# A two-layer encoder trunk on one core: mean squares as columns, and four modulation products beside the norms

## The reference

```python
mod = silu(c) @ mod_w[i] + mod_b[i]              # 1024 -> 6 * 1024
sh1, sc1, g1, sh2, sc2, g2 = split(mod, 6)
h = rms_norm(x, g) * (1 + sc1) + sh1
x = x + g1 * mixer(h)                            # layer 0: sparse attention; layer 1: S5 state space, GELU, GLU
h = rms_norm(x, g') * (1 + sc2) + sh2
x = x + g2 * (silu(gate) * val) @ w_down         # val, gate: causal convolution (width 3) of h @ w_up, 2816 channels each
```

## Time and profile before

| | us |
|---|---|
| timed runs | 835.84, 837.55, 838.05 |
| median | 837.55 |
| span of the profiled execution | 833.9 |
| TensorE busy | 757.5 (91%) |
| TensorE weight load busy | 681.9 (82%) |
| VectorE busy | 579.9 (70%) |
| ScalarE busy | 389.2 (47%) |
| GpSimd busy | 209.6 (25%) |

### The profile page before, as it was taken

The page is one execution under the profiler, slowest core; times in us unless marked ns, Lnnn a source line. Parts: engine busy times, 40 slices in busy tenths (PEclk is TensorE's granted clock), DMA queues, the critical chain, the costliest instruction groups (busy, mean ns, idle before and its releaser), DMA issues.

```text
span 833.9 us, 17636 instructions
## 1 busy us (share of the span) xinstructions
PE 757.5 (91%) x6676; PEld 681.9 (82%) x6676; DVE 579.9 (70%) x935; ACT 389.2 (47%) x651; POOL 209.6 (25%) x121
## 2 busy tenths in 40 slices
PE   4588999999877888999999968997999999999996
PEld 0177999558666877999999958997988999999995
DVE  7854655995689998565565787567657766666775
ACT  2255544555333434444544724332556555555553
POOL 6900000211899995000001063364000000000000
PEclk9789999999859989999999969999998999999998
DMA  8869555696315646677866412110552555555521
GB/s 310 344 222 387 180 177 177 252 407 264 138 44 208 225 153 220 237 276 264 276 254 239 149 51 77 53 53 28 190 187 79 181 197 176 181 177 189 183 101 52
DMA packets 45978, 157.51 MB, mean 189 GB/s; under 512 B 6256, under 2 KB 7792, under 8 KB 45936
## 3 DMA queue, kind: packets, MB, share of 16 engines
q1 hardware_dynamic: 43632, 148.55, 51.5%
q10 hardware_dynamic: 1728, 6.29, 1.9%
q0 software_dynamic: 576, 2.10, 0.7%
HBM read 155.87 MB, written 1.05 MB: 188 GB/s over the span
## 4 chain that ended last, share of the span: by engine, by line
PE 71%; DVE 18%; ACT 4%; issue 3%; DMA 2%; POOL 1%; DVEq 0%; ACTq 0%; POOLq 0%
PE up L326 12%; PE up L328 12%; PE up L327 12%; PE acc L326 8%; PE acc L327 8%; PE acc L328 8%; DVE wlo L978 4%; DVE hl L1007 3%; PE gv L362 3%; DVE ffn L1237 2%; DMA ffn<-in_mw 1%; DVE ffn L1232 1%; ACT whi L719 1%; DVE diag L999 1%; PE misc L373 1%
## 5 line engine op out<-in xcount | busy, mean ns | idle before, releaser
L978 DVE TENSOR_TENSOR wlo<-raw,whi 128x1024 fp32r<-128x1024 f32 x194 | 256.2, 1332 | 117.8 <-ACT whi L719 116.6
L326 PE MATMUL up<-hh,whi 128*128 128x256 f32 x944 | 276.2, 293 | 16.2 <-DVE hl L1007 10.8
L327 PE MATMUL up<-hl,whi 128*128 128x256 f32 x944 | 272.3, 288 | 0.0
L328 PE MATMUL up<-hh,wlo 128*128 128x256 f32 x944 | 272.1, 288 | 0.0
L719 ACT ACTIVATE whi<-raw 128x1024 fp32r<-128x1024 f32 x194 | 201.1, 1051 | 50.2 <-PE up L328 25.2
L326 PEld LDWEIGHTS up<-hh,whi 128*128 128x128 f32 x944 | 186.2, 197 | 30.3 <-DVE wlo L978 14.0
L327 PEld LDWEIGHTS up<-hl,whi 128*128 128x128 f32 x944 | 186.9, 198 | 0.0
L328 PEld LDWEIGHTS up<-hh,wlo 128*128 128x128 f32 x944 | 186.6, 198 | 0.0
L1232 DVE SCALAR_TENSOR_TENSOR ffn<-up,conv,ffn 128x254 f32<-128x254 f32 (+1 forms) x176 | 72.6, 474 | 55.3 <-ACT ffn L853 55.3
L326 PE MATMUL acc<-ah,whi 128*128 128x256 f32 x352 | 102.1, 290 | 8.0 <-DVE wlo L978 8.0
L327 PE MATMUL acc<-al,whi 128*128 128x256 f32 x352 | 101.8, 289 | 0.0
(11 more groups left out here) (200 smaller groups left out, 947.0 us busy)
## 6 DMA issues: line engine op xcount, KB each, us to landing
raw<-in_w SPq DMA_DIRECT2D x194, 512.0 KB, 4.1
mraw<-in_mw SPq DMA_DIRECT2D x60, 512.0 KB, 6.1
arena<-in_mw SPq DMA_DIRECT2D x12, 512.0 KB, 10.8
tmp<-in_mw SPq DMA_DIRECT2D x6, 512.0 KB, 7.9
ffn<-in_mw SPq DMA_DIRECT2D x6, 512.0 KB, 8.5
tmp<-in_mw ACTq DMA_DIRECT2D x4, 512.0 KB, 7.4
ffn<-in_mw ACTq DMA_DIRECT2D x4, 512.0 KB, 9.6
mraw<-in_mw ACTq DMA_DIRECT2D x4, 512.0 KB, 14.6
```

The lines of the kernel that those rows point to most:

```text
L326: pe.matmul(out, w_h, xh, start=first, stop=False, skip_group_check=skip)
L327: pe.matmul(out, w_h, xl, start=False, stop=False, skip_group_check=skip)
L328: return pe.matmul(out, w_l, xh, start=False, stop=last, skip_group_check=skip)
L978: dve.tensor_tensor(wlo[:, n % SPL, :], raw[:, n % RAW, :], whi[:, n % SPL, :].bitcast(F32), ALU.subtract).then_inc(lo_ready, 1)
```

## The change

The mean squares: instead of rows of sums, each squared tile is now the stationary operand. For each half of 128 tokens it is multiplied by one column that holds 1/1024 everywhere (the new small input mean), and the eight tiles are added up in two columns of misc. The row copy on ScalarE, the turning products and their two semaphores are gone. TensorE's waits for the columns of the modulation now stand ahead of the sums.

The products: 14 runs within norm 1 between the sums and the spread, 15 after the spread; 22 and 23 do the same at norm 3. Product 15 has a place of its own in the arena (fill), loaded when attention has ended; 22 and 23 are loaded after the state space (mraw and late). The loop of layer 0 has a product in its first six iterations only, 16 to 21. The sets of columns move along: one stands ahead of each layer's loop. GpSimd waits for product 15 before it writes over its place.

```diff
+C_LAST = 2 * CH - 2
+FILLED = C_LAST - C_FFN - 2
 ...
 # SP
             load_att(C_FFN)
-            for n in range(W_OUT + RAW, W_FFN0 + RAW):
+            load_w(W_OUT + RAW)
+            for s in range(MS):
+                if s == 0:
+                    sp_.wait_ge(act_lo, 2 * KT)
+                sp_.dma_start(fill[:, s, :], t["mw"][(C_FFN + 1) * MS + s, :, :]).then_inc(m_fill[s], 16)
+            for n in range(W_OUT + RAW + 1, W_FFN0 + RAW):
                 load_w(n)
-            with sp_.Fori(0, 9) as i:
+            with sp_.Fori(0, FILLED) as i:
                 for n in range(W_FFN0 + RAW, W_FFN0 + 2 * RAW):
                     load_w(n, i)
-                load_m(C_FFN + 1, i)
+                load_m(C_FFN + 2, i)
 ...
+            for s in range(2 * MS):
+                if s == 0:
+                    sp_.wait_ge(y_done, KT)
+                sp_.dma_start(mraw[:, s, :] if s < MS else late[:, s - MS, :],
+                              t["mw"][C_LAST * MS + s, :, :]).then_inc((m_loaded if s < MS else m_fill)[s % MS], 16)
 ...
 # TensorE
-            def norm(n, pairs, spread, meanwhile=None):
-                pe.wait_ge(gm_ready, pairs)
+            def norm(n, spread, meanwhile=None):
+                pe.wait_ge(cols_done, 1 if n == 0 else C_FFN // 2 if n == 1 else CH - 1 if n < 4 else CH)
+                pe.wait_ge(mod_col, 1 if n == 0 else C_FFN // 2 if n == 1 else CH - 1 if n < 4 else CH)
                 for k in range(KT):
                     pe.wait_ge(sq_ready, KT * n + k + 1)
-                    mm = pe.matmul(gv[32 * (k % 4):32 * (k % 4) + 1, 0:T], ones[:, 0:1], tmp[:, k, :],
-                                   start=(k < 4), stop=(k >= 4))
+                    for h in range(2):
+                        mm = pe.matmul(misc[:, 8 + h:9 + h], tmp[:, k, h * P:(h + 1) * P], mean[:],
+                                       start=(k == 0 and h == 0), stop=(k == KT - 1), skip_group_check=True)
                 mm.then_inc(ssum, 1)
-                pe.wait_ge(sum_row, n + 1)
-                pe.wait_ge(mod_col, pairs)
-                for h in range(2):
-                    mm = pe.matmul(misc[:, 8 + h:9 + h], gm[:, h * P:(h + 1) * P], picks[:, 0:1], start=True, stop=True)
-                mm.then_inc(csum, 1)
                 if meanwhile:
                     meanwhile()
 ...
-            norm(1, C_FFN // 2, misc[:, T:2 * T])
+            norm(1, misc[:, T:2 * T], lambda: gemv(C_FFN))
+            gemv(C_FFN + 1)
 ...
+                columns(C_FFN // 2 if layer == 0 else CH - 1)
                 if layer == 0:
-                    with pe.Fori(0, 5) as i:
-                        gemv(C_FFN, i)
+                    with pe.Fori(0, FILLED // 2) as i:
+                        gemv(C_FFN + 2, i)
                         two_steps(2 * i)
-                        gemv(C_FFN + 1, i)
+                        gemv(C_FFN + 3, i)
                         two_steps(2 * i + 1, i)
+                    with pe.Fori(FILLED, 10) as i:
+                        two_steps(i)
 ...
-            norm(3, CH, misc[:, T:2 * T])
+            norm(3, misc[:, T:2 * T], lambda: gemv(C_LAST))
+            gemv(C_LAST + 1)
 ...
 # ScalarE, root
-                act.wait_ge(cols_done, 1 if norm == 0 else C_FFN // 2 if norm == 1 else CH)
-                act.activation(gm[:, 0:T], gv[:, 0:T], ACT.Copy).then_inc(sum_row, 1)
-                act.wait_ge(csum, norm + 1)
-                act.activation(rt[:], misc[:, 8:10], ACT.Sqrt, scale=1.0 / D, bias=epsc[:, 0:1]).then_inc(rt_ready, 1)
+                act.activation(rt[:], misc[:, 8:10], ACT.Sqrt, bias=epsc[:, 0:1]).then_inc(rt_ready, 1)
 ...
 # GpSimd
+                if k == 1:
+                    pool.wait_ge(mod_used, (C_FFN + 2) * MS)
 ...
-            pool.wait_ge(mod_used, 2 * CH * MS)
+            pool.wait_ge(mod_used, C_LAST * MS)
```

More of the change, by code:

```diff
@@ L182, in build @@
         qkv_f = arena[:, 0:N_IN * T]
+        fill = arena[:, 12288:16384].rearrange("p (s n) -> p s n", n=1024)
+        late = arena[:, 0:4096].rearrange("p (s n) -> p s n", n=1024)
         hh_f = hh[:].rearrange("p k t -> p (k t)")
@@ L202, in build @@
         m_early = [sem(f"m_early{j}") for j in range(3 * MS)]
-        sum_row, csum = sem("sum_row"), sem("csum")
+        m_fill = [sem(f"m_fill{j}") for j in range(MS)]
         x_in = sem("x_in")
@@ L297, in _ @@
             load_att(C_FFN)
-            for n in range(W_OUT + RAW, W_FFN0 + RAW):
+            load_w(W_OUT + RAW)
[4 more added lines that the diff above has]
+            for n in range(W_OUT + RAW + 1, W_FFN0 + RAW):
                 load_w(n)
-            with sp_.Fori(0, 9) as i:
+            with sp_.Fori(0, FILLED) as i:
                 for n in range(W_FFN0 + RAW, W_FFN0 + 2 * RAW):
                     load_w(n, i)
-                load_m(C_FFN + 1, i)
-            for n in range(W_FFN0 + 10 * RAW, W_FFN0 + 11 * RAW):
-                load_w(n)
-            for n in range(W_SIN, W_SIN + 3):
-                load_w(n)
-            first = W_SIN + 3
+                load_m(C_FFN + 2, i)
+            with sp_.Fori(FILLED, 10) as i:
+                for n in range(W_FFN0 + RAW, W_FFN0 + 2 * RAW):
+                    load_w(n, i)
+            for n in range(W_SIN, W_GLU + 8):
+                load_w(n)
+            for s in range(2 * MS):
[3 more added lines that the diff above has]
+                              t["mw"][C_LAST * MS + s, :, :]).then_inc((m_loaded if s < MS else m_fill)[s % MS], 16)
+            first = W_GLU + 8
             loops = (N_SLOTS - first) // RAW
@@ L346, in gemv @@
                     src = mraw[:, s, :]
-                    if c >= C_FFN:
-                        pe.wait_ge(m_loaded[s], 16 * (c - C_FFN // 2 + 2 * i))
+                    if c in (C_FFN + 1, C_LAST + 1):
+                        src = (fill if c == C_FFN + 1 else late)[:, s, :]
+                        pe.wait_ge(m_fill[s], 16 if c == C_FFN + 1 else 32)
+                    elif c == C_FFN:
+                        pe.wait_ge(m_loaded[s], 16 * (c // 2))
+                    elif c > C_FFN:
+                        pe.wait_ge(m_loaded[s], 16 * (c - C_FFN // 2 - 1 + 2 * i))
                     elif c == 0:
@@ L431, in _ @@
             columns(0)
-            norm(0, 1, None)
+            norm(0, None)
             gemv(2)
@@ L608, in _ @@
             lag_kernels(range(0, 5))
-            norm(2, CH, misc[:, T:2 * T], lambda: lag_kernels(range(5, KT - 1)))
+            norm(2, misc[:, T:2 * T], lambda: lag_kernels(range(5, KT - 1)))
             lag_kernels(range(KT - 1, KT)).then_inc(k_done, 1)
@@ L707, in _ @@
             pe.wait_ge(set_up, 5)
-            norm(3, CH, misc[:, T:2 * T])
+            norm(3, misc[:, T:2 * T], lambda: gemv(C_LAST))
+            gemv(C_LAST + 1)
             ffn_phase(1, W_FFN1, 5)
-            norm(4, CH, misc[:, T:2 * T])
+            norm(4, misc[:, T:2 * T])
         @block.scalar
@@ L899, in ffn_phase @@
                 for h in range(2):
-                    step(h, 20 + h, base + 60 + 3 * h, 0, 4 if layer == 0 and h == 0 else None)
+                    step(h, 20 + h, base + 60 + 3 * h)
             act.wait_ge(small_in, 16 * N_SMALL)
@@ L1271, in two_steps @@
                         step(h, 2 * i + 2 + h, base + 6 + 3 * h, i, extra if h else None)
+                col_out(C_FFN // 2 if layer == 0 else CH - 1)
                 if layer == 0:
-                    with dve.Fori(0, 4) as i:
+                    with dve.Fori(0, FILLED // 2) as i:
                         two_steps(2 * i)
                         two_steps(2 * i + 1, i)
-                    two_steps(8)
+                    with dve.Fori(FILLED, 9) as i:
+                        two_steps(i)
                 else:
@@ L1281, in ffn_phase @@
                 for h in range(2):
-                    step(h, 20 + h, base + 60 + 3 * h, 0, 4 if layer == 0 and h else None)
+                    step(h, 20 + h, base + 60 + 3 * h)
                 if layer == 0:
@@ L1566, in layout @@
         "ones": np.ones((P, P), f),
+        "mean": np.full((P, 1), 1.0 / D, f),
         "picks": np.stack([np.arange(P) % 32 == 0, np.arange(P) % 32 == 1], axis=1).astype(f),
```

18 lines of the change are left out of this document (11 added, 7 removed).

## The result

The changed kernel takes 894.0 us (median of four runs, 893.49 to 895.72) against 836.7 (835.36 to 838.05) for the kernel before, timed beside it: a ratio of 1.069, 95% interval 1.067 to 1.071, or 57.3 us more. The forecast was 892, range 866 to 907. Its profiled execution has a span of 893.9, that of before 833.9.

What follows compares the result with a forecast made beforehand. TensorE's sequence of matmuls plus its waits was taken as the bound. Stalls 60, products -7.3 and norms +2.1 gave +54.8 on the 833.9 span, 888.7; with 3.65 around it 892.35, say 892 us, range 866 to 907.

Steps and rivals of the forecast that it cites:

- stalls in six iterations: Layer 0's feed-forward loop: TensorE waits for late product loads, 36 us in iterations 3 to 5, 24 in 0 to 2: +60.
- four products out of the loop: Layer 0's loop, iterations 6 to 9: four fewer products of 1.83 us on TensorE's chain give back 7.3 us.
- norms: All five norms with column sums: -0.9 at norm 1, -0.5 at 3, +0.8, +0.2 and +2.5 at 2, final and 0; +2.1.
- moved loads: End of attention and after the state space: loads moved past others are covered, 0 us, at most 2 if served late.
- The clock's price: Layer 0's loop: after each stall TensorE restarts at 1.2 GHz, costing 2 us each, bounds 0 and 2.9.
- the strict reading of the lock: Norm 0: VectorE and GpSimd exclude each other for whole instructions, costing 4.5 us instead of 2.5; time 894.
- the loads come in time: Rival, layer 0's loop: SP is an iteration ahead, stalls vanish, 832 us; decided by a lead of 8 us; chance 0.07.
- The shorter stalls: Rival, layer 0's loop: loads land quicker while TensorE is still and the clock holds, 36 us, 866 to 870; chance 0.14.
- No cover in the early iterations: Rival, layer 0's first iterations: VectorE is the bottleneck, delays come on top, 60 + 15, about 907 us; chance 0.08.
- The idle times: Sign in layer 0's first six iterations: TensorE idle before the products until transfers into mraw land, 8 to 12 us each.
- the iterations of 30 and 17.5 us: Sign in layer 0's loop: iterations of about 31 us, then four of about 17.5.
- A clock of 0.5 behind each stall: Sign in layer 0's loop: TensorE's granted clock would be 0.5 behind each stall.

Runs made afterwards that it cites:

- experiment 1: The changed kernel with product 16 loaded ahead of SP's loop and 17 + i in iteration i, restoring the lead: 840.1 us, ratio 1.004.
- experiment 5: Kernel before with products moved, lead restored, norms by rows, plus two weight slots issued ahead of SP's wait for attention's end: 827.6 us, ratio 0.988.
- experiment 4: Two kernels against the one before: only the new column sums, 843.7 us; only the products moved, lead restored and norms by rows, 831.0 us.
- the first group: The first of three groups in which the eleven follow-up kernels ran, each beside the kernel before, whose median there was 836.3 us.
- experiment 7: experiment 1 with norm 0's sums in another PSUM bank, ahead of the wait for the columns: 836.5 us, ratio 0.999 to the kernel before.
- experiment 3: The changed kernel with the product's four loads behind five, three or none of SP's six weight slots: 870.9, 843.6 and 841.7 us.
- behind three slots: The changed kernel with the product's loads behind three of SP's six weight slots in layer 0's loop: 843.6 us, ratio 1.008.

## Why the prediction was right, and where it was not

The mechanism is right: the kernel got slower because SP's product loads lost their iteration of lead. That the total was only 2 us off is luck. The stalls were put 6 to 7 us too high, the norms 7 and the moved loads 3 too low, and these errors nearly cancelled.

| term | forecast | trace of the changed kernel | difference of kernels |
|---|---|---|---|
| stalls in six iterations | +60 | +53.1 | +53.9 (experiment 1) |
| four products out of the loop | -7.3 | -8.5 | -8.6 (experiment 5, with all the moved work) |
| norms | +2.1 | +10.5, with products 14 and 22 in them | +9.1 (experiments 1 and 4; +7.3 alone) |
| moved loads | 0, at most 2 | | +3.3 (experiments 4 and 5) |

The last column sums to 57.7 against 57.3, but that confirms nothing: its terms are steps from one kernel to the next, from the changed kernel back to the one before, and add up to the whole whatever each is due to. The 0.4 is the difference between the medians of the kernel before, beside the changed kernel and in the first group.

**The stalls, over by 7.** For iterations 3 to 5 I forecast 12 each: 9.8 idle and 2 for the clock behind it. They cost 10.8, 10.5 and 9.7. The product ended at arrival + 12.4, against the forecast 11.6, so the place and the landing were right. The clock's price was in the wrong place: it fell on the product, while the pieces trickled in, and was largely hidden under the wait for the last piece. The slots behind it cost nothing: in all six iterations the granted clock is 1.00 there. One row was misread for it: the matmul of 0.39 us still ran at full clock, 1.00 from 268.3 to 269.0. At full clock the first matmul of a slot shows 0.38 (406.10), at half clock 0.58 (297.69). In iteration 0 the error has the other sign: 15.4 instead of 8.6. The product ended 14.0 us later than it would have (277.8, arrival 262.0, less 1.8), and nothing covered it: a wait for VectorE as long as the one that I had set against it, 4.28 us, stands at 297.69, later in the iteration. VectorE had not worked on while TensorE stood. From 274.7 to 282.04 it waited 7.33 us for a split of ScalarE's, which waited for TensorE to use a slot; before, its longest such wait in the iteration was 0.5. Iterations 1 and 2 then cost only 2.3 and 4.4 instead of 8.6 and 7. GpSimd does work on while TensorE stands: of the 63.6 us that it had left, the first iteration holds 39.9 and the third none, where before the three had 25.1, 27.5 and 16.6. So the cover lay in the next two iterations, which had been slow beside GpSimd and no longer were. The three together: 22.1 against 24.2, and this agreement too is luck.

**The products, right.** The last four iterations gave 8.5. Two sets of columns of 0.95 us also left them, which I had booked as zero since they go elsewhere: 7.3 + 1.9 would be 9.2.

**The norms, under by 7.** I assumed that sums whose squares come one by one run one by one too, so that in norms 1 and 3 only the last tile would count. TensorE does its instructions in order, and the sums stand behind the last projection. At norm 3 all 32 run in one burst of 3.63 us, which ends 2.0 us after the last square; the old chain needed 1.76 from there to the root, so the 1.08 us won with the row copy went back. At norm 1 they were won: 28 of the 32 end before the last square, which is late there, and the root starts 0.69 us behind the square instead of 1.76. But product 14 ran at half clock (3.46 us) and held the spread until 231.32, though the diagonals were ready at 229.02. The price of a burst was right (forecast 3.5 at full clock and 7 at half, measured 3.6 and 6.95), but norms 2 and 4 ran theirs at a clock of 0.90 and 0.79, in 4.1 and 4.5. Norm 0 had +2.5 and measured +4.6. It was the strict reading of the lock that came true. The Trainium skill, SBUF: State Buffer, section Two separate sides, has a GpSimd instruction and a VectorE instruction that uses the shared ports (one in a 2-port mode or with two inputs from SBUF) exclude each other for whole instructions. The diagonals agree: they end within 0.3 us of GpSimd's instruction in both kernels, and experiment 7 shows the price from the other side. The table load of 1.28 us was a term that I did not have. Before, it ran while TensorE waited for the first columns; after, it stands in the open.

**The moved loads, under by 3.** I named the cover (seven slots with their weights) and did not count when ScalarE wants the eighth: it waited 5.08 us. The second price came through TensorE's clock at norm 1, which the traces of experiment 5 show.

**The rivals.** That the loads come in time fell with the first row of waits; its condition, a lead of 8 us, is what experiment 3 found (7.3 us ahead left 1.5 us, 9.0 left 0.2). The shorter stalls by the figures of the Trainium skill (DMA: Bandwidth & Descriptors, Anatomy of one DMA) did not occur: the transfers took what the trace before had shown, 6.8 to 7.3 us for the fourth, and the stalls of iterations 3 to 5 cost 9.7 to 10.8. No cover in the early iterations fell as well, but only for the three together: they cost 22.1 us, where three uncovered ones would cost some 31 at the price of the later iterations. The first alone had no cover.

**The signs.** The idle times came, 5.1 to 10.4 us where 8 to 12 were named, and the iterations of 30 and 17.5 us. A clock of 0.5 behind each stall came only in the product. The loop became 44.6 us longer (53.1 less 8.5) instead of some 50.

Open: why three of the kernels with column sums (experiments 1 and 7, and behind three slots) scatter by 7 to 12 us over ten runs, where the other new kernels scatter by 1.5 to 5.6 over two to six. The mean granted clock goes with it: in experiment 1 the runs of 835.2 and 836.9 us had 0.944 and 0.945, those of 841.0 to 842.2 had 0.934 to 0.936. What makes the clock differ from run to run is not shown.

## What to carry to other kernels

A prefetch in an in-order queue has a lead that is set by its place in the queue, not by the moment at which its buffer comes free. Whoever takes a consumer out of a loop must move the loads of the remaining ones forward by as many, or each iteration pays the latency in full; here one line before the loop was worth 54 us. And look for a second price behind a late transfer, in what TensorE then runs at half clock. At norm 1 it was larger than the delay itself (2.8 us against 1.6), where a chain of dependent steps stood; in the loop it was mostly hidden under the wait for the last piece.

## What the runs showed of the hardware that was not expected

Behind waits of 5.1 to 10.4 us for the transfers the granted clock was 0.50 in the product's first pieces and 1.00 in the slot behind it, in all six iterations. The product took 4.9 to 6.4 us instead of 1.9. At half clock with all its pieces there it takes 3.5; the rest is that it ran piece by piece. A piece alone took 1.03 us at full clock and 1.87 at half, where four together take 1.9 at full clock.

The mean squares as columns, 32 matmuls that each stream one column past 128 x 128 float32 weights, take 3.63 us at full clock, 0.11 each, and 6.95 at half. A matmul of a projection, which streams 256 columns of the rounded type, takes 0.12. One column instead of 256 won next to nothing there, though the types differ.

Four loads of 512 KB issued within 2.1 us landed 4.1 to 7.3 us after their issue, when TensorE stood still beside them too.
